# Two feed-forward sublayers of a decoder step, each as seven products of quarters instead of eight

## The chip, the cores and the metric

One core of a Trainium2 chip runs the whole kernel. The metric is the time of one execution on the device in microseconds (us): the median of several runs, lower is better. Beside it stands one profiled execution, from which all durations below are read.

## The reference

One layer of a decoder trunk is computed for 512 prompt tokens and 32 sample tokens (544 columns, handled together). It is a feed-forward sublayer, a mixing sublayer (differential attention and retention side by side), and a second feed-forward sublayer, each followed by a layer norm. The part that matters here is computed twice, with `D_MODEL` = 1024 and `D_FF` = 2816:

```python
def swiglu(x, w_gu, w_down):
    a, u = jnp.split(x @ w_gu, 2, axis=-1)
    return (jax.nn.silu(a) * u) @ w_down

def ffn_sublayer(x, w_gu, w_down, g, b):
    return layer_norm(ALPHA * x + 0.5 * swiglu(x, w_gu, w_down), g, b)
```

## The kernel before

Activations lie with channels on the 128 partitions and the 544 tokens along the free axis (`xT`: 8 tiles of 128 channels). Every large product is done in three passes: weight and activation are each split into a rounded high part (`fp32r`) and the rest, and TensorE (PE) adds high times high, high times low and low times high. A chunk of weights is 256 columns of a matrix and up to 8 tiles of 128 rows, 1 MB. SP loads it (`load_chunk`, line 270) into one of two buffers of `w_raw`, ScalarE (ACT) makes the high part (`split_hi`, line 276), VectorE (DVE) subtracts to get the low part (`split_lo`, line 281), and `gemm` (line 289) multiplies: for each row tile three passes, in each of them one matmul for either half of the tokens (272 columns), into two banks of PSUM. Buffers are handed on by counters: `lo_split` frees the raw chunk, `gemm_done` the split one.

`FFN` (line 315) has two stages. The upper one loops 11 times over a chunk of the gate half and one of the up half of `w_gu`: PE makes two gate tiles and two up tiles, ACT takes the silu of the gate tiles out of PSUM (line 373), DVE multiplies the up tiles by it (line 394), and the product is split again into `hh` and `hl` (lines 377 and 397). The lower one goes through 12 chunks of `w_down`; DVE adds the result, scaled, to `xT` (line 413) and, in the first sublayer, adds the finished tiles into `x_sum` for the norm (line 603). At the end of the first sublayer the next two chunks, those of the projection `pk`, are already loaded and split. GpSimd (POOL) does nothing in either sublayer.

`ChannelNorm` (line 571) follows the first sublayer and the mixing sublayer: PE sums over channels with a matrix of ones (lines 608 and 614), DVE takes a reciprocal (line 642) and scales the 8 tiles (line 646), ACT adds the bias twice, once rounded into `xh` (line 633) and once into `xT` (line 634), and DVE makes `xl` (line 651). The first `gemm` behind it starts on a tile as soon as that tile's `xl` is there. Ahead of the first sublayer `turn_in` turns the input with PE, ACT writes it to `xT` and `xh` (lines 501 and 502) and DVE makes `xl` (line 546). Behind the second one `ln3` turns the result back and stores it.

Each engine runs its own list of instructions in order; an instruction that waits for a counter holds up all that stand behind it on its engine.

## Time and profile before

| | |
|---|---|
| median of 3 runs | 1947.2 us (1946.07 to 1953.2) |
| span of the profiled execution | 1943.7 us |
| matmuls with their records in the trace | 13247 |
| busy: PE, DVE, ACT, POOL | 93%, 40%, 34%, 4% |
| first sublayer, first matmul to last | 27.9 to 426.4 us |
| second sublayer, first matmul to last | 1519.4 to 1921.2 us |

The span runs from the first to the last instruction of the profiled execution; the timed runs have some 3.5 us more at the median. "Busy" is the share of the span in which an engine had at least one instruction running; matmuls overlap one another, so the time of a stream of them is read from its length and its count, not from the duration of one.

### The profile page before, as it was taken

How to read it: one execution, taken by the hardware profiler on the slowest of the kernel's cores; microseconds unless marked ns; L12 is line 12 of the kernel's file. 1: busy time of each engine (PE TensorE's matmuls, PEld its weight loads, DVE VectorE, ACT ScalarE, POOL GpSimd, SP SyncE). 2: the span in 40 equal slices, each digit the busy share in tenths (PEclk: the TensorE clock that was granted, in tenths of full speed). 3: DMA queues.
4: the chain of work that ended last, by engine and by line, in shares of the span. 5: the costliest groups of instructions: out<-in, count | busy, mean ns of one | idle time of the engine just before them, and what ended most of it. 6: DMA issues, size and time to landing. Idle time of an engine off the chain costs nothing.

```text
span 1943.7 us, 33105 instructions
## 1 busy us (share of the span) xinstructions
PE 1804.9 (93%) x13247; PEld 1699.9 (87%) x13247; DVE 778.9 (40%) x1081; ACT 667.4 (34%) x899; POOL 85.2 (4%) x113
## 2 busy tenths in 40 slices
PE   6999999998997768999989999999999899999996
PEld 5999999987997537878768999869998799999996
DVE  2333332234223875756663223344345433333123
ACT  3333331124223555666563222124322433332111
POOL 0000000000002420000000000110000000000002
PEclk9999999999997998999989999999999999999998
DMA  4222222230440015767752232062223022222221
GB/s 142 91 90 91 89 84 82 81 108 22 133 133 23 1 51 176 273 228 249 242 169 91 87 98 84 17 215 66 91 91 100 22 86 87 89 90 84 92 97 46
DMA packets 146659, 203.75 MB, mean 105 GB/s; under 512 B 5538, under 2 KB 127330, under 8 KB 146594
## 3 DMA queue, kind: packets, MB, share of 16 engines
q1 hardware_dynamic: 145442, 198.35, 31.4%
q0 software_dynamic: 1152, 4.46, 0.6%
q8 instruction: 49, 0.80, 0.2%
q14 instruction: 16, 0.13, 0.0%
HBM read 191.39 MB, written 11.40 MB: 104 GB/s over the span
## 4 chain that ended last, share of the span: by engine, by line
PE 88%; DVE 4%; ACT 4%; issue 2%; DMA 0%; SPq 0%; POOL 0%; ACTq 0%; POOLq 0%; DVEq 0%
PE ps L297 68%; PE ps L1201 4%; PE ps L1232 3%; PE ps L1187 2%; PE ps L974 1%; PE ps L988 1%; PE ps L614 1%; PE ps L1624 1%; PE ps L1211 1%; PE ps L1616 1%; PE ps L1248 1%; PE ps L699 1%; PE ps L1198 1%; ACT aT L1069 1%; PE ps L981 0%
## 5 line engine op out<-in xcount | busy, mean ns | idle before, releaser
L297 PE MATMUL ps<-xh,w_hi_t 128*128 128x272 f32 x2432 | 510.1, 291 | 25.3 <-DVE xl L651 18.3
L297 PE MATMUL ps<-xh,w_lo_t 128*128 128x272 f32 x2432 | 505.9, 290 | 0.0
L297 PE MATMUL ps<-xl,w_hi_t 128*128 128x272 f32 x2432 | 504.2, 289 | 0.0
L283 DVE TENSOR_TENSOR w_lo_t<-w_raw,w_hi_t 128x2048 fp32r<-128x2048 f32 (+1 forms) x112 | 252.4, 2254 | 519.2 <-ACT w_hi_t L279 519.2
L297 PEld LDWEIGHTS ps<-xh,w_hi_t 128*128 128x128 f32 x2432 | 385.0, 190 | 30.2 <-issue 20.7
L297 PEld LDWEIGHTS ps<-xl,w_hi_t 128*128 128x128 f32 x2432 | 385.1, 190 | 0.0
L297 PEld LDWEIGHTS ps<-xh,w_lo_t 128*128 128x128 f32 x2432 | 382.4, 190 | 0.0
L279 ACT CAST w_hi_t<-w_raw 128x2048 fp32r<-128x2048 f32 (+1 forms) x112 | 209.9, 1874 | 276.5 <-PE ps L297 276.5
L297 PE MATMUL ps<-hh,w_lo_t 128*128 128x272 f32 x704 | 145.7, 288 | 0.0
L297 PE MATMUL ps<-hh,w_hi_t 128*128 128x272 f32 x704 | 145.5, 288 | 0.0
L297 PE MATMUL ps<-hl,w_hi_t 128*128 128x272 f32 x704 | 145.1, 288 | 0.0
L297 PEld LDWEIGHTS ps<-hh,w_hi_t 128*128 128x128 f32 x704 | 110.7, 188 | 0.0
L297 PEld LDWEIGHTS ps<-hl,w_hi_t 128*128 128x128 f32 x704 | 110.6, 189 | 0.0
L297 PEld LDWEIGHTS ps<-hh,w_lo_t 128*128 128x128 f32 x704 | 109.9, 189 | 0.0
L1303 DVE TENSOR_TENSOR kt_lo<-ps,kt_hi 128x512 fp32r<-128x512 f32 x128 | 82.5, 685 | 57.3 <-ACT kt_hi L1302 57.1
L377 ACT CAST hh<-prod 128x544 f32 x44 | 28.6, 649 | 216.0 <-DVE prod L394 216.0
L1302 ACT CAST kt_hi<-ps 128x512 fp32r<-128x512 f32 x128 | 70.3, 587 | 66.9 <-PE ps L1187 66.7
L1187 PE MATMUL ps<-ident,k_page 128*128 128x128 f32 x512 | 74.8, 285 | 14.1 <-DVE kt_lo L1303 12.4
L1324 DVE TENSOR_TENSOR vp_lo<-v_page,vp_hi 128x1024 fp32r<-128x1024 f32 x64 | 76.4, 1222 | 19.3 <-ACT vp_hi L1320 18.9
L1187 PEld LDWEIGHTS ps<-ident,k_page 128*128 128x128 f32 x512 | 57.5, 144 | 29.1 <-DVE kt_lo L1303 12.8
L394 DVE TENSOR_TENSOR prod<-ps,gated 128x544 f32<-128x544 f32 x44 | 31.9, 725 | 108.2 <-PE ps L297 108.2
L1201 PE MATMUL ps<-kt_hi,q_stat 128*128 128x256 f32 x256 | 71.9, 314 | 0.0
(245 smaller groups left out, 2107.0 us busy)
## 6 DMA issues: line engine op xcount, KB each, us to landing
w_raw<-in_ffn_w_gu_dram SPq DMA_DIRECT2D x44, 1024.0 KB, 5.1
w_raw<-in_w_in_dram SPq DMA_DIRECT2D x32, 1024.0 KB, 5.7
k_page<-in_cache_k_dram SPq DMA_DIRECT2D x64, 512.0 KB, 4.8
v_page<-in_cache_v_dram SPq DMA_DIRECT2D x64, 512.0 KB, 4.6
w_raw<-in_ffn_w_down_dram SPq DMA_DIRECT2D x16, 1024.0 KB, 5.1
w_raw<-in_ffn_w_down_dram SPq DMA_DIRECT2D x8, 768.0 KB, 4.7
w_raw<-in_w_branch_a_dram SPq DMA_DIRECT2D x4, 1024.0 KB, 5.2
st_in<-in_state_ret_dram SPq DMA_DIRECT2D x8, 512.0 KB, 5.0
```

What stands on the lines that cost most here:

```text
L279: nc.scalar.copy(w_hi_t[:, j, 0:nk], w_raw[:, j, 0:nk]).then_inc(hi_split, 1)
L283: nc.vector.tensor_tensor(w_lo_t[:, j, 0:nk], w_raw[:, j, 0:nk], w_hi_t[:, j, 0:nk].bitcast(F32), ALU.subtract).then_inc(lo_split, 1)
L297: mm = nc.tensor.matmul(ps[:, bank + half, 0:HALF], w[:, j, k, w_cols], m[:, k0 + k, half * HALF:half * HALF + HALF], start=start and k == ...
L377: nc.scalar.copy(hh[:, bass.ds(2 * i + n, 1)], prod[:, n:n + 1]).then_inc(self.h_hi, 1)
L394: nc.vector.tensor_tensor(halves(prod[:, n]), banks(4 + 2 * n), halves(gated[:, n]), ALU.mult).then_inc(self.prod_done, 1)
L614: mm = nc.tensor.matmul(ps[:, 2 + a, 0:HALF], ones[:], x_sq[:, k % 2, a * HALF:a * HALF + HALF], start=k == 0, stop=k == KD - 1)
L1187: mm = nc.tensor.transpose(ps[:, half, h * P:h * P + P], k_page[:, g % 4, (4 * half + h) * P:(4 * half + h) * P + P], ident[:])
L1201: mm = nc.tensor.matmul(dst, q_stat[:, P * h:P * h + P], kt[:, q % 2, h], start=False, stop=h == HA - 1 and kt is kt_lo)
L1232: mm = nc.tensor.matmul(ps[:, 6 + half, :], pT[:, g], v[:, g % 2, 512 * half:512 * half + 512], start=g == 0 and v is vp_hi, stop=False)
L1302: return nc.scalar.copy(at_hi, src)
L1303: return nc.vector.tensor_tensor(at_lo, src, at_hi.bitcast(F32), ALU.subtract)
L1324: nc.vector.tensor_tensor(vp_lo[:, g % 2], v_page[:, g % 4], vp_hi[:, g % 2].bitcast(F32), ALU.subtract).then_inc(self.v_lo, 1)
```

## The change

A product of two matrices cut into 2 x 2 quarters normally takes eight products of quarters; Strassen's scheme (here in Winograd's form) takes seven and some additions of quarters. Both sublayers are rewritten in it. A **unit** is 256 columns of weights: 11 `g` units (gate) and 11 `u` units (up), each 1024 rows deep, and 16 `d` units (down) in four groups of four, 2, 3, 3 and 3 pairs of row tiles deep. The quarters of a unit's weights are even and odd row tiles by left and right 128 columns; those of the activations are even and odd row tiles by the two halves of the tokens. The 38 units are worked in the order g0 u0 g1 u1 g2 u2, four d, three pairs, four d, three pairs, four d, two pairs, four d.

A product is 3 passes over 4 (or 2 or 3) row tiles with 272 columns: 12 (6, 9) matmuls into one bank of PSUM. `P1`, `P2`, `P4` take quarters of weights as they are; `P5`, `P6`, `P7`, `P3` take sums of quarters, which POOL makes (`weight_sum`). ACT and DVE split each of the seven into high and low (ring of `SLOTS` = 6). The activations' seven operands are made once per sublayer for g and u (`pool_x`, `act_x`, `dve_x`) and once per pair for d (`hc_hi`, `hc_lo`). Intermediate sums are carried in PSUM and by drains on ACT (copies after P1, P5, P6), DVE (additions after P2, P7, P3, P4) and POOL (the gate's products and the four operand sums after P7 and P3 of a u unit; three additions into `xT` of each d unit). The products of neighbouring units are mixed, so that between a product and the one that needs its drain stand others: for unit n the steady order is P1(n+1) P2(n+1) P7(n) P5(n+1) P3(n) P4(n) P6(n+1). Only the last u unit goes straight into d units that need it.

Besides: `xh` and `xl` are no longer made at the input and by the second `ChannelNorm`; the first two chunks of `pk` are loaded behind the first sublayer, and split inside the norm behind it; the loops of the sublayers are written out.

```diff
+    for lo, hi in ((0, 2), (2, 5), (5, 8), (8, KF // 2)):
+        while pairs < min(hi + 1, KF // 2):
+            units += [("g", pairs, 0, KP), ("u", pairs, 0, KP)]
+            pairs += 1
+        units += [("d", m, lo, hi) for m in range(4)]
...
+            entries += [whole(n + 1, "P1"), whole(n + 1, "P2"), whole(n, "P7"), whole(n + 1, "P5"),
+                        whole(n, "P3"), whole(n, "P4"), whole(n + 1, "P6")]
...
+            def pe_part(self, pe):
+                for e, (n, q, k0, k1) in enumerate(self.entries):
+                    s = self.slot_of[n, q]
+                    pe.wait_ge(self.w_lo, self.s0 + s + 1)
+                    kind, _, lo, _ = self.units[n]
+                    if kind == "d":
+                        pe.wait_ge(self.h_lo, KF // 2 * self.i + k1)
+                    elif n < 2:
+                        pe.wait_ge(self.x_lo, 7 * self.i + B_OF[q] + 1)
...
+                    elif q == "P7":
+                        pe.wait_ge(self.u2_kept, self.n0 + n + 1)
+                        dst = self.x_bank(n)
+                    elif q == "P4":
+                        pe.wait_ge(self.c22, self.n0 + n + 1)
+                        dst = self.x_bank(n)
...
+                        for t, (wt, m) in enumerate(((a_hi, b_hi), (a_hi, b_lo), (a_lo, b_hi))):
+                            mm = nc.tensor.matmul(dst, wt, m, start=opens and k == k0 and t == 0,
+                                                  stop=k == k1 - 1 and t == 2, skip_group_check=True)
+                    mm.then_inc(self.product, 1)
...
+            def weight_sum(self, pool, n, q):
+                self.raw_ready(pool, n)
+                if n:
+                    pool.wait_ge(self.w_lo, self.s0 + self.slot_of[n - 1, P_OF[q]] + 1)
+                out = f_sum[:, int(q) - 1, 0:self.depth(n)]
...
+                    nc.gpsimd.tensor_tensor(out, self.raw(n, 0, 1), self.raw(n, 1, 1), ALU.add).then_inc(self.w_sum, 1)
...
+            def pool_x(self, pool):
...
+                self.x_ready(pool)
+                nc.gpsimd.tensor_tensor(t1, self.quarter(0, 1), self.quarter(0, 0), ALU.subtract).then_inc(self.x_sum4, 1)
...
+                nc.gpsimd.tensor_tensor(t2, self.quarter(1, 1), t1, ALU.subtract).then_inc(self.x_sum4, 1)
...
+                nc.gpsimd.tensor_tensor(t4, self.quarter(1, 0), t2, ALU.subtract).then_inc(self.x_sum4, 1)
+                nc.gpsimd.tensor_tensor(t3, self.quarter(1, 1), self.quarter(0, 1), ALU.subtract).then_inc(self.x_sum4, 1)
...
+            def dve_part(self, dve):
+                for s in range(SLOTS):
+                    self.split_lo(dve, s)
+                self.dve_x(dve)
+                for e in range(len(self.entries)):
+                    self.dve_drain(dve, e)
+                    for p in range(KF // 2):
+                        if e == self.hidden_entry(p, 5):
+                            self.dve_hidden(dve, p)
...
+                    for s in self.split_at[e]:
+                        self.split_lo(dve, s)
...
+            def hidden_entry(self, p, later):
+                e = self.done[self.unit_of["u", p, KP], "P4"] - 1
+                return e if p == KF // 2 - 1 else e + later
...
             def act_part(self, act):
...
+                    self.act_drain(act, e)
+                    for p in range(KF // 2):
+                        if e == self.done[self.unit_of["g", p, KP], "P3"]:
+                            self.act_gate(act, p)
+                        if e == self.hidden_entry(p, 3):
+                            self.act_hidden(act, p)
+                    for s in self.split_at[e]:
+                        self.split_hi(act, s)
...
+                        nc.gpsimd.tensor_tensor(b12[:], b12[:], gate[:, i % 2, 2], ALU.mult).then_inc(self.h_mul, 1)
...
+                        nc.gpsimd.tensor_tensor(t[:, 2], b12[:], t[:, 0], ALU.subtract).then_inc(self.h_sum, 1)
+                        nc.gpsimd.tensor_tensor(t[:, 4], t[:, 6], b12[:], ALU.subtract).then_inc(self.h_sum, 1)
...
+                        nc.gpsimd.tensor_tensor(t[:, 3], t[:, 6], t[:, 2], ALU.subtract).then_inc(self.h_sum, 1)
...
+                        nc.gpsimd.tensor_tensor(t[:, 5], t[:, 1], t[:, 3], ALU.subtract).then_inc(self.h_sum, 1)
...
+                if self.split:
+                    split_hi(act, 0, 0, 0)
+                    split_hi(act, 1, 0, 1)
                 for k in range(KD):
                     act.wait_ge(self.scaled, KD * self.i + k + 1)
...
                 scale(0)
                 scale(1)
+                if self.split:
+                    split_lo(dve, 0, 0)
+                    split_lo(dve, 1, 1)
```

An entry is a product in the list that PE works through. `split_at` gives entry e the splits of the operand six products on, whose place in the ring the product at e has freed; POOL makes the sum for the next unit as soon as the same sum of this unit is split (`weight_sum`). So the operands run five products ahead of PE.

## Rows read from the trace of the kernel before

**Rows 1.** The page, part 1: busy us, share of the span, instructions
```profile
PE 1804.9 (93%) x13247; PEld 1699.9 (87%) x13247; DVE 778.9 (40%) x1081; ACT 667.4 (34%) x899; POOL 85.2 (4%) x113
```

**Rows 2.** The page, part 4: the chain that ended last, by line
```profile
PE ps L297 68%; PE ps L1201 4%; PE ps L1232 3%; PE ps L1187 2%; PE ps L974 1%; PE ps L988 1%; PE ps L614 1%; PE ps L1624 1%; PE ps L1211 1%; PE ps L1616 1%; PE ps L1248 1%; PE ps L699 1%; PE ps L1198 1%; ACT aT L1069 1%; PE ps L981 0%
```

**Rows 3.** The chain in order of time: start us, us, what, times
```profile
27.86 398.54 PE ps L297 x3168
...
565.90 42.10 PE ps L297 x336
...
782.10 1.85 PE ps L1232 x8
...
1529.29 391.90 PE ps L297 x3126
```

**Rows 4.** Stretches of both sublayers: busy us (instructions) by engine, granted clock, DMA
```profile
31.20:426.50 395.30, 395.19 (x3155) 394.97 (x3153) 114.89 (x92) 101.11 (x89) 0.00 (x0) 1.00 0.27 88
1533.00:1921.50 388.50, 388.18 (x3099) 387.96 (x3097) 108.50 (x84) 98.59 (x86) 0.00 (x0) 1.00 0.25 81
```

**Rows 5.** Groups by line and shape, DVE and ACT: busy us, mean ns
```profile
L283 DVE TENSOR_TENSOR w_lo_t<-w_raw,w_hi_t 128x2048 fp32r<-128x2048 f32 x104 | 238.4, 2292 | 448.2 <-ACT w_hi_t L279 448.2
L397 DVE TENSOR_TENSOR hl<-prod,hh 128x544 f32 x44 | 31.9, 726 | 40.9 <-ACT hh L377 40.9
L1668 DVE SCALAR_TENSOR_TENSOR st_out<-st_in,ps 128x256 f32<-128x256 f32 x32 | 11.3, 415 | 23.6 <-PE ps L1624 23.6
L279 ACT CAST w_hi_t<-w_raw 128x2048 fp32r<-128x2048 f32 x104 | 198.0, 1904 | 198.2 <-PE ps L297 198.2
L377 ACT CAST hh<-prod 128x544 f32 x44 | 28.6, 649 | 216.0 <-DVE prod L394 216.0
```

**Rows 6.** Groups by line and shape, POOL
```profile
L568 POOL TENSOR_TENSOR xn<-xn,ln_bias 128x1024 f32<-128x1024 f32 x4 | 9.4, 2345 | 639.8 <-ACT xn L508 639.8
L1691 POOL TENSOR_TENSOR qx<-qrT,cross 128x512 f32<-128x512 f32 x3 | 3.8, 1269 | 6.2 <-PE ps L1587 3.8 <-PE ps L1584 2.4
```

**Rows 7.** Timeline of the attention stage, its start and a later moment: DVE and POOL
```profile
610.57 2.29 DVE L283 TENSOR_TENSOR w_lo_t<-w_raw,w_hi_t 128x2048 fp32r<-128x2048 f32 x1 [9.72 <-ACT w_hi_t L279]
612.78 0.62 DVE L1418 TENSOR_TENSOR qs_lo<-qaT,qs_hi 128x256 fp32r<-128x256 f32 x1
613.32 0.83 DVE L1421 TENSOR_TENSOR kn_lo<-kaT,kn_hi 128x256 fp32r<-128x256 f32 x1
...
610.95 2.17 POOL L958 TENSOR_TENSOR bias<-dist,small 128x128 f32<-128x128 f32 x1 [1.16 <-DVEq L1101]
613.08 0.79 POOL L953 TENSOR_TENSOR q_stage<-qaT,small 128x256 f32<-128x256 f32 x1
613.83 0.58 POOL L958 TENSOR_TENSOR bias<-dist,small 128x128 f32<-128x128 f32 x1
614.45 0.60 POOL L953 TENSOR_TENSOR q_stage<-qaT,small 128x256 f32<-128x256 f32 x1
615.02 0.39 POOL L958 TENSOR_TENSOR bias<-dist,small 128x128 f32<-128x128 f32 x1
...
703.05 0.61 POOL L953 TENSOR_TENSOR q_stage<-qaT,small 128x256 f32<-128x256 f32 x1 [1.72 <-PE ps L974]
...
703.11 0.69 DVE L1020 CUSTOM_DVE_ANT_0 s_sb<-ps,bias 128x512 f32<-128x512 f32 x1
...
703.72 0.69 DVE L1020 CUSTOM_DVE_ANT_0 s_sb<-ps,bias 128x512 f32<-128x512 f32 x1
```

**Rows 8.** Timeline around the second norm: DVE
```profile
1498.58 2.29 DVE L283 TENSOR_TENSOR w_lo_t<-w_raw,w_hi_t 128x2048 fp32r<-128x2048 f32 x1 [0.24 <-ACT w_hi_t L279]
...
1512.71 3.55 DVE L642 RECIPROCAL x_rs<-x_rs 128x544 f32<-128x544 f32 x1 [6.79 <-ACT x_rs L629]
1516.30 1.48 DVE L646 SCALAR_TENSOR_TENSOR xT<-xT,ln_cols,x_rs 128x544 f32<-128x544 f32 x2
```

**Rows 9.** Timeline around the first norm: DVE
```profile
443.33 3.55 DVE L642 RECIPROCAL x_rs<-x_rs 128x544 f32<-128x544 f32 x1 [7.47 <-ACT x_rs L629]
446.92 1.48 DVE L646 SCALAR_TENSOR_TENSOR xT<-xT,ln_cols,x_rs 128x544 f32<-128x544 f32 x2
...
449.15 0.73 DVE L651 TENSOR_TENSOR xl<-xT,xh 128x544 fp32r<-128x544 f32 x1 [0.76 <-ACT xT L634]
```

**Rows 10.** Timeline at the start: the input's way through ACT
```profile
20.00 1.01 ACT L501 COPY xT<-ps 128x1024 f32<-128x1024 f32 x1 [0.22 <-PE ps L474]
20.91 1.02 ACT L502 CAST xh<-ps 128x1024 fp32r<-128x1024 f32 x1
```

**Rows 11.** The page, part 6: DMA issues, KB each, median us to landing
```profile
w_raw<-in_ffn_w_gu_dram SPq DMA_DIRECT2D x44, 1024.0 KB, 5.1
v_page<-in_cache_v_dram SPq DMA_DIRECT2D x64, 512.0 KB, 4.6
```

More of the change, by code:

```diff
@@ L263, in build @@
         out_stored = sem("out_stored")
+        rows_landed = [sem(f"rows_landed{j}") for j in range(4)]
         def score_ps(row):
@@ new lines, in build @@
+            raw_in = [sem(f"f_raw_in{j}") for j in range(RAWS)]
+            w_sum, w_hi, w_lo = sem("f_w_sum"), sem("f_w_hi"), sem("f_w_lo")
+            product = sem("f_product")
+            x_sum4, x_hi, x_lo = sem("f_x_sum"), sem("f_x_hi"), sem("f_x_lo")
+            u1_kept, p5_kept, u2_kept = sem("f_u1_kept"), sem("f_p5_kept"), sem("f_u2_kept")
+            c11, c22, c12 = sem("f_c11"), sem("f_c22"), sem("f_c12")
+            c21_act, c21_dve = sem("f_c21_act"), sem("f_c21_dve")
+            gated = sem("f_gated")
@@ new lines, in build @@
+            h_mul, h_sum, h_hi, h_lo = sem("f_h_mul"), sem("f_h_sum"), sem("f_h_hi"), sem("f_h_lo")
+            added = sem("f_added")
+            units, entries = ffn_plan()
+            N = len(units)
+            slot_of, done = {}, {}
+            for e, (n, q, _, _) in enumerate(entries):
+                slot_of.setdefault((n, q), len(slot_of))
+                done[n, q] = e + 1
+            slots = list(slot_of)
+            sum_of = {(0, q): j + 1 for j, q in enumerate("1234")}
+            for n, q in slots:
+                if q in SUM_OF and n + 1 < N:
+                    sum_of[n + 1, SUM_OF[q]] = len(sum_of) + 1
@@ new lines, in build @@
+            split_at = [[] for _ in entries]
+            for s in range(SLOTS, len(slots)):
+                e = max(done[slots[s - SLOTS]] - 1, max([k for k, got in enumerate(split_at) if got], default=0))
+                split_at[e].append(s)
+            c21_of, n_act, n_dve, d_of = {}, 0, 0, {}
+            for n, unit in enumerate(units):
+                if unit[0] == "g":
+                    n_act += 1
+                    c21_of[n] = n_act
+                else:
+                    n_dve += 1
+                    c21_of[n] = n_dve
+                if unit[0] == "d":
+                    d_of[n] = len(d_of)
@@ new lines, in build, with __init__ @@
+            added_of = {}
+            for n, q, _, k1 in entries:
+                if n in d_of and q in ("P2", "P7", "P3") and k1 == units[n][3]:
+                    added_of[n, q] = len(added_of) + 1
+            unit_of = {(u[0], u[1], u[3]): n for n, u in enumerate(units)}
+            def __init__(self, index, w_gu, w_down, x_ready, free, norm=None):
+                self.i, self.gu, self.down = index, w_gu, w_down
+                self.x_ready, self.free, self.norm = x_ready, free, norm
+                self.n0, self.p0, self.s0 = self.N * index, len(self.entries) * index, len(self.slots) * index
@@ new lines, in kind, with depth, made, c21_read @@
+            def kind(self, n):
+                return self.units[n][0]
+            def depth(self, n):
+                return self.units[n][3] - self.units[n][2]
+            def made(self, eng, n, q):
+                eng.wait_ge(self.product, self.p0 + self.done[n, q])
+            def c21_read(self, eng, n):
+                if self.kind(n) == "g":
+                    eng.wait_ge(self.c21_act, self.n_act * self.i + self.c21_of[n])
+                else:
+                    eng.wait_ge(self.c21_dve, self.n_dve * self.i + self.c21_of[n])
@@ new lines, in hidden_free, with out @@
+            def hidden_free(self, eng, p):
+                if p >= PAIRS:
+                    part = next(u for u in self.units if u[0] == "d" and u[2] <= p - PAIRS < u[3])
+                    self.made(eng, self.unit_of["d", 3, part[3]], "P4")
+            def out(self, n, c):
+                kind, i, _, _ = self.units[n]
+                j = {"11": 0, "22": 1, "12": 2}[c]
+                if kind == "g":
+                    return gate[:, i % 2, j]
+                if kind == "u":
+                    return b12[:] if c == "12" else hc_raw[:, i % PAIRS, {"11": 0, "22": 6}[c]]
+                return self.scratch(n, j)
@@ L1542, in __init__ @@
                 self.s_sc_set = sem("rs_sc_set")
-                self.s_in = [sem(f"rs_in{j}") for j in range(4)]
+                self.s_in = rows_landed
                 self.s_qm_zero = sem("rs_qm_zero")
@@ L1799, in act_part @@
             def act_part(self, act):
-                with act.Fori(0, 2) as i:
-                    for j in range(2):
-                        split_hi(act, self.c + 2 * i + j + 2, self.c // 2 + i + 1, j)
+                for j in range(2):
+                    split_hi(act, self.c + j + 2, self.c // 2 + 1, j)
             def dve_part(self, dve):
@@ L1842, in build @@
         out_proj = OutProject(C_OUT)
-        ln2 = ChannelNorm(1)
-        ffn2 = FFN(1, C_FFN2_UP, ffn2_w_gu, ffn2_w_down, last=True)
-        ln3 = Norm(2, 0, 1, back=False)
+        ln2 = ChannelNorm(1, split=False)
+        ffn2 = FFN(1, ffn2_w_gu, ffn2_w_down, ln2.ready, lambda eng: eng.wait_ge(gemm_done, 2 * C_END + 4))
+        ln3 = Norm(2)
         att_const = sem("att_const")
@@ L2082, in _ @@
             ln2.pe_part(pe)
-            ffn2.pe_part(pe, lambda k: ln2.ready(pe, k))
-            pe.wait_ge(ffn2.resid, 2 * KD + 4)
+            ffn2.pe_part(pe)
+            for m in range(4):
+                ffn2.settled(pe, m)
             ln3.pe_part(pe)
```

611 lines of the change are left out of this document (391 added, 220 removed).

## The prediction, made before the changed kernel ran

> **What bounds the kernel now.** I read the page first: PE is busy 93% of the span, DVE 40%, ACT 34%, POOL 4% [rows 1], and line 297, the large products, is 68% of the chain that ended last [rows 2]. The chain in order of time shows both sublayers as one unbroken piece of PE each: 3168 matmuls in 398.5 us and 3126 records in 391.9 us [rows 3], so 0.1254 us for each at full pace (391.9 / 3126). Over these stretches the granted clock is 1.00, the 2.4 GHz level, DVE and ACT work 29% and 26% of the time and POOL not at all [rows 4]. So PE's count of matmuls sets both sublayers, some 797 of 1943.7 us, and fewer matmuls are worth time as long as the others keep up. That is the question, because the change gives them more.
>
> **What is removed.** A unit g or u took 96 matmuls and takes 84, a pair of row tiles of a d block 24 and now 21. A sublayer goes from 3168 to 22 x 84 + 4 x 11 x 21 = 2772, so 396 x 0.1254 = 49.7 us less for either, 99.3 us together. Two doubts about PE cost next to nothing. Twelve matmuls in a row now go into one bank: line 1232 does that, with 512 columns, in 0.231 us each (1.85 / 8), 0.45 ns a column, as 0.1254 us for 272 is 0.46 [rows 3]. And the code is unrolled: `pq`, unrolled too, runs 336 matmuls in 42.1 us, 0.1253 each [rows 3].
>
> **What is added.** Prices, from groups with the same operands [rows 5, 6]:
> - DVE with two SBUF inputs: 2048 elements 2.29 us, 544 0.73; in between 0.16 + 1.04 ns each, so 512 (a split) 0.69, 384 0.56, 256 0.43, 1088 1.29, 1904 (the hidden operands of a pair) 2.14. DVE with one PSUM input, 256 elements 0.415; the drains of 272 I take at 0.4, as they overlap a little.
> - ACT: 2048 1.90, 544 0.65, so 0.20 + 0.83 ns: 512 0.62 (0.55 in a row), 272 0.4, 1904 1.8, 816 0.87.
> - POOL with two full inputs: 1024 2.35, 512 1.27, so 0.19 + 2.10 ns: 384 1.00, 272 0.76, 256 0.73, 1088 2.48.
>
> PE needs 10.5 us for a unit g or u (84 x 0.1254), 7.9 for a d unit 3 deep, 5.3 for one 2 deep. Taken alone every engine fits: for g and u DVE 7.5 us, ACT 6.5, POOL 4 x 1.27 + 3.5 x 0.76 = 7.7. The loads fit too: 1 MB in 5.1 us [rows 11], asked for about a unit ahead.
>
> **DVE and POOL exclude each other.** This decides the sum, and the trace has one place that shows it [rows 7]. POOL's line 958 takes 0.39 us when left alone (615.02). At 610.95 it begins beside a split of DVE and takes 2.17: it ends at 613.12, 0.26 behind the end of the split (612.86). DVE's next subtraction of 256 elements ends at 613.40, 0.28 behind that, instead of taking 0.43; then POOL at 613.87, DVE at 614.15, POOL at 614.41. Each waits for the other to finish a whole instruction, in turn. What is held is the price less a start of 0.14 us: POOL 1.13 for 512, 0.86, 0.62 (272), 0.59, 2.34; DVE 0.55, 0.42, 0.28, 1.15, 2.0. Drains out of PSUM go free: line 1020, with one input there, takes 0.69 beside POOL (703.11) as alone (703.72).
>
> The Trainium skill, "SBUF — State Buffer", section "Who interferes with whom", says that a DVE instruction with two SBUF inputs and a GpSimd instruction that reads SBUF lock each other out through a shared read port, while one with a single SBUF input does not; the first half agrees with the 2.17 us [rows 7], and by the page's reading the sum below holds, without it the first rival does.
>
> Held time, which has to follow one after the other:
> - pair g + u: POOL 8 x 1.13 + 7 x 0.62 = 13.4, DVE 14 x 0.55 + 2.0 = 9.7: 23.1 us, against 21.1 of PE and 24.1 before (192 x 0.1254).
> - d 3 deep: 4 x 0.86 + 3 x 0.62 + 7 x 0.42 = 8.2, against 7.9 and 9.0 before. 2 deep: 4 x 0.59 + 1.86 + 7 x 0.28 = 6.2, against 5.3 and 6.0.
>
> So not PE sets the pace but this pair of engines. Nor can they fill every moment. I laid two pairs out, each instruction at the price above behind what it waits for. POOL's burst of a u unit (two products, five operations, three sums) makes DVE wait for one of them at every split. The last operand sum comes 7 us behind P4 of u; ACT, in order, waits for it with `act_hidden` and its next split behind it; DVE waits for that split, and behind it stands the addition after P7, for which PE waits at P4: 1.4 us in the u unit, 2.0 in the g unit. A pair comes to 24.6 us, 1.5 over the held time; one d unit to 8.7 and 6.7. Stream of a sublayer: 11 x 24.6 + 12 x 8.7 + 4 x 6.7 = 401.8, less 3 for the first pair, which starts without arrears, plus 2 for the larger sums of g and u made beside the shallow d: 401, against 397.3 (3168 x 0.1254). **+4 each, +8.** From below the bound is the held time filled without gaps, 11 x 23.1 + 12 x 8.2 + 4 x 6.2 = 377; from above, whole prices one behind the other (13.4, 9.9, 7.9 a unit), 445.
>
> **Ends and joints.**
> - From u10 into the d units PE has no other work, where before it had no gap [rows 3]. Behind P4: POOL's five operations, in arrears by 3 us, end 6.5 us later, then the cast 1.8, DVE's subtraction 2.1: 10.5 us, of which 1.5 come back as arrears are made up. **+18** for both; without arrears 6.7 each.
> - Start of the second sublayer. Before, PE began behind the reciprocal (ended 1516.26 [rows 8]) while tiles were still coming; had it run at full pace it would have begun at 1529.29 - 42 x 0.1254 = 1524.0, 7.8 us behind it. After: eight tiles scaled and biased to +6.6, six splits on ACT to +9.8, then POOL's four sums of activations (2.34 held) and DVE's seven splits of them (1.15 held) in turn: the fifth operand, for P7, is there at +27.9, with six products (9.0 us) done by then. 27.9 - 9.0 - 7.8 = **+11**; if they didn't exclude each other +6.
> - Start of the first: ACT's copies take a tile each 1.0 us less [rows 10], so x is ready at 22.3; by the same steps P7 starts at 43.6, so 43.6 - 9.0 = 34.6 against 29.1 before (27.86 + 398.54 - 397.3 [rows 3]). **+5.5**; PE will be idle in between, and if it gets the 1.2 GHz level for that, up to 3 more.
> - First norm into `pk`: two weight chunks are split inside it. ACT's two casts (3.8) lie beside the reciprocal (3.55 [rows 9]) and cost nothing; DVE's two (4.5) go before the first `xl`, which began 0.75 us behind the scaling [rows 9], so 3.75 late, less 0.85 for the split that used to stand before the centring. Their loads are queued on SP behind the end of the sublayer and take 2 x 5.1 us, hidden by 20 us of norm. **+2.9.** DVE's eight additions for the norm now compete in the last d units: **+2**. Second norm: one split less before it [rows 8], **-0.5**.
> - The end keeps its length: the last drains are shorter, POOL's lie beside P4.
>
> Sum: 8 + 18 + 11 + 5.5 + 2.9 + 2 - 0.5 = +47 on 1943.7, so a span of 1990.6; the runs' median stands 3.5 above the span: **1994 us**, 2.4% slower. (A measurement of this kernel can tell some 0.5% from no change, 1937.5 to 1957.)
>
> **The rivals.**
> - *They hardly meet* (faster). If the exclusion is rare in practice, PE sets the pace: -99.3, + 2 x 6.7 at u10, + 1 and + 6 at the starts, + 2.4 at the norms, + 7 for stalls behind the hidden casts in the shallow d units: -69.5, 1878 us. For it: each engine alone has a third of its time free. Against it: every split and every POOL operation here is of the kind in rows 7. 0.17.
> - *They meet but fill every moment*: 377 instead of 401 (-20 each instead of +4), u10 +13, starts +12, norms +2.4: -13, 1934 us; with some of the gaps, up to 1957. For it: arrears of five products are allowed for. Against it: P4 waits for the addition two products behind P7. 0.15, half of it within 0.5%.
> - *It doesn't even reach turn-taking* (slower still): whole prices in sequence, 445 a sublayer, +96 and +40 for the rest: 2083 us. It decides if an engine never has its next instruction waiting when the other lets go; rows 7 show it waiting each time. 0.05.
> - That fewer products are computed by count is plain from the code; no chance for that.
>
> **How the numbers follow.** The forecast has 0.63: 1957 to 2045, from gaps half as large to twice as large (3 us a pair more is +66). The most likely time is 1994. The range 1905 to 2045 leaves out the first rival, the third, and little else. Faster by over 0.5%: 0.17 + 0.07 = 0.24; within: 0.08 + 0.02 of the forecast's lower edge = 0.10; slower: 0.66.
>
> **What would show it.** PE busy in the sublayers falls from 100% to about 86%, with some 5540 matmuls at 0.125 us inside a product. PE's waits are on DVE's additions (`c22`, before P4) and, at u10, on the hidden split. DVE's splits of 512 elements show 0.9 to 1.8 us instead of 0.69, and POOL's sums more than 1.27; if they read 0.69 and 1.27, the forecast is wrong and the first rival right. A pair takes 24.6 us from P1 to P1; the gap behind the last P4 of u is 10 us; the second sublayer's P7 starts 28 us behind the reciprocal.

## The result, and the profile after

The changed kernel takes 2054.2 us (2053.1 to 2055.7, four runs) against 1950.2 before: 1.053 times as long, interval 1.0505 to 1.0554. The direction was forecast, the size was not: +47 us on the span were expected, 110 came (2053.9 against 1943.7), and 2054 lies 9 us above the range.

The page of after: busy time by engine, PE and POOL in 40 slices, and the chain by engine (before: [rows 1, 2]).

```profile
PE 1761.9 (86%) x12455; PEld 1637.9 (80%) x12455; DVE 1261.4 (61%) x1746; ACT 874.5 (43%) x1550; POOL 748.5 (36%) x675
...
PE   4979898876999776999989999899995888889885
...
POOL 4777777761100430000000000210002677777765
...
PE 61%; DVE 16%; issue 10%; ACT 6%; POOL 6%; DMA 0%; SPq 0%; ACTq 0%; POOLq 0%; DVEq 0%
```

PE has 792 matmuls fewer, and POOL is now busy 36% of the span instead of 4%, nearly all of the added time in the sublayers. There the chain no longer stays on PE; it runs through DVE, ACT and POOL as well. The two stretches from the seventh product (P7 of the first unit) to the last matmul of a sublayer, after (length, then busy us and instructions of PE, PEld, DVE, ACT, POOL, granted clock, DMA; before: [rows 4]):

```profile
52.00:475.90 423.90, 361.06 (x2702) 351.25 (x2700) 335.10 (x414) 198.12 (x401) 306.96 (x269) 0.97 0.23 75
1610.80:2031.70 420.90, 361.06 (x2702) 351.75 (x2700) 330.42 (x408) 198.08 (x400) 306.34 (x269) 0.97 0.24 78
```

PE is busy 85% (361.06 / 423.90). The forecast had 86%, but that the two agree is luck: 2702 matmuls at 0.1254 us are 339 us, or 80%. The rest is time at a lower clock (0.97 granted, 1.00 before) and, at each wait, a last matmul whose record is longer than its share of a stream (0.29 against 0.126 us).

The next rows are DVE's splits (count; minimum, median and maximum in ns) and POOL's sums (busy us, mean ns) after; in the timeline, POOL takes 1.27 us for such a sum while DVE is idle, and DVE 0.68 for a split.

```profile
L557 DVE TENSOR_TENSOR f_lo<-f_sum,f_hi x176: 675/1142/1783, 24.9 to 1980.1; 128x512 fp32r<-128x512 f32 x176
L557 DVE TENSOR_TENSOR f_lo<-f_raw,f_hi x132: 676/896/1777, 23.7 to 1981.5; 128x512 fp32r<-128x512 f32 x132
...
L579 POOL TENSOR_TENSOR f_sum<-f_raw,f_sum 128x512 f32<-128x512 f32 x44 | 67.4, 1532 | 5.5 <-POOL f_sum L567 4.8 <-issue 0.7
L572 POOL TENSOR_TENSOR f_sum<-f_sum,f_raw 128x512 f32<-128x512 f32 x44 | 58.3, 1326 | 23.9 <-DVE f_lo L557 19.1 <-DVE f_lo L554 3.0 <-POOL f_sum L579 1.0
```

The splits begin at 0.68 us (the 0.69 of the sum) and reach 1.78, which is one POOL sum held (1.13) and one split held (0.55) on top of a tenth; the sums are at 1.33 to 1.53 instead of 1.27. So the splits and sums take as long as the exclusion priced them. Where the other 63 us come from, by the forecast's own terms (times of the first and last matmuls of products and sublayers in both traces):

| term | forecast, us | measured | over |
|---|---|---|---|
| first sublayer: P7 of unit 0 starts at | 43.6 | 52.0 | +8.4 |
| first sublayer: from there to its last matmul | 403.3 | 423.9 | +20.6 |
| first norm into `pk` | +2.9 | +3.9 | +1.0 |
| `pk` to the end of the output projection (unchanged code) | 0 | +8.8 | +8.8 |
| second norm up to its reciprocal | -0.5 | -3.0 | -2.5 |
| second sublayer: P7 behind the reciprocal | 27.9 | 35.5 | +7.6 |
| second sublayer: from there to its last matmul | 401.0 | 420.8 | +19.8 |
| end | 0 | -0.3 | -0.3 |

(403.3 is 426.4 of before + 5.5 + 4 + 9 + 2 - 43.6; 401.0 is 404.9 from reciprocal to last matmul before + 11 + 4 + 9 - 27.9.) Measured from P1 to P1, the inner pairs take 23.7 and 24.0 us in the mean (forecast 24.6), but a d unit 3 deep 10.9 (8.7) and one 2 deep 9.1 and 8.6 (6.7). In a group 3 deep the four come as 10.3, 13.2, 9.6 and 10.6 us. (The last group, behind u10, is left out of these means.)

One thing the sum had only at the starts is the clock. 0.03 short of full speed is 24 to 25 us at the 1.2 GHz level in each sublayer from P7 on, most of it in the groups of d units, where PE waits most. Three pairs in a row of after, and then a group of four d units, as above:

```profile
143.50:214.00 70.50, 63.10 (x487) 61.95 (x487) 57.97 (x66) 34.60 (x67) 51.93 (x41) 0.99 0.25 83
214.00:257.60 43.60, 35.88 (x264) 34.53 (x263) 35.07 (x45) 19.35 (x42) 34.61 (x32) 0.96 0.26 85
```

88 and 94 matmuls begin at that level in the two sublayers. They start 0.23 us apart instead of 0.126, some 9 us more of PE's time in each sublayer; how much of it lies on the path, inside the 20 us of the table, no run separates.

What goes on in a d unit of after, from 242.7 us on: ACT, DVE and POOL.

```profile
245.92 0.39 ACT L715 COPY gate<-ps 128x272 f32<-128x272 f32 x1 [3.68 <-POOL xT L776]
246.21 1.35 ACT L545 ACTIVATE f_hi<-f_sum 128x384 fp32r<-128x384 f32 x3
...
244.44 0.76 DVE L554 SCALAR_TENSOR_TENSOR f_lo<-f_raw,f_hi 128x384 fp32r<-128x384 f32 x1
246.77 0.56 DVE L554 SCALAR_TENSOR_TENSOR f_lo<-f_sum,f_hi 128x384 fp32r<-128x384 f32 x1 [1.56 <-ACT f_hi L545]
...
242.75 1.01 POOL L572 TENSOR_TENSOR f_sum<-f_sum,f_raw 128x384 f32<-128x384 f32 x1 [0.55 <-DVE f_lo L554]
243.72 1.07 POOL L764 TENSOR_TENSOR xT<-xT,gate 128x272 f32<-128x272 f32 x1
244.75 1.08 POOL L776 TENSOR_TENSOR xT<-xT,gate 128x272 f32<-128x272 f32 x1
247.47 1.01 POOL L575 TENSOR_TENSOR f_sum<-f_raw 128x384 f32<-128x384 f32 x1 [1.63 <-DVE f_lo L554]
```

ACT's drain of P5 (line 715) stands 3.68 us for POOL's addition of the unit before (776), because the scratch it writes is read there. Three splits queue behind the drain, DVE idles 1.56 us for them, POOL idles 1.63 us for DVE. That is a ring of three in-order queues, and no step of the sum had it.

### The profile page after: what moved, and what is told of

Read it like the earlier page. It is cut to its first block, busy times and chain, and to the rows that moved or that the text cites. A ratio compares the mean times of both kernels' runs of the same rounds, so it can differ in the third digit from the quotient of the medians.

```text
span 2053.9 us, 34447 instructions
## 1 busy us (share of the span) xinstructions
PE 1761.9 (86%) x12455; PEld 1637.9 (80%) x12455; DVE 1261.4 (61%) x1746; ACT 874.5 (43%) x1550; POOL 748.5 (36%) x675
## 4 chain that ended last, share of the span: by engine, by line
PE 61%; DVE 16%; issue 10%; ACT 6%; POOL 6%; DMA 0%; SPq 0%; ACTq 0%; POOLq 0%; DVEq 0%
PE ps L338 26%; PE ps L525 16%; DVE f_lo L557 4%; DVE f_lo L554 4%; PE ps L1570 3%; PE ps L1601 3%; PE ps L1556 2%; DVE hc_lo L664 2%; PE ps L1343 2%; ACT f_hi L545 1%; PE ps L1357 1%; DVE gate L643 1%; PE ps L1617 1%; PE ps L975 1%; PE ps L1995 1%
## 5 line engine op out<-in xcount | busy, mean ns | idle before, releaser
L525 PE MATMUL ps<-xc_hi,f_hi 128*128 128x272 f32 x1232 | 364.7, 296 | 83.0 <-DVE xc_lo L612 35.2
L525 PE MATMUL ps<-xc_hi,f_lo 128*128 128x272 f32 x1232 | 360.6, 293 | 0.0
L525 PE MATMUL ps<-xc_lo,f_hi 128*128 128x272 f32 x1232 | 359.2, 292 | 0.0
L525 PEld LDWEIGHTS ps<-xc_hi,f_hi 128*128 128x128 f32 x1232 | 236.4, 192 | 93.0 <-issue 46.9
L525 PEld LDWEIGHTS ps<-xc_lo,f_hi 128*128 128x128 f32 x1232 | 236.6, 192 | 0.0
L525 PEld LDWEIGHTS ps<-xc_hi,f_lo 128*128 128x128 f32 x1232 | 236.2, 192 | 0.0
L338 PE MATMUL ps<-xh,w_hi_t 128*128 128x272 f32 x1024 | 217.5, 294 | 15.0 <-DVE xl L1016 12.9
L338 PE MATMUL ps<-xh,w_lo_t 128*128 128x272 f32 x1024 | 214.4, 291 | 0.0
L338 PE MATMUL ps<-xl,w_hi_t 128*128 128x272 f32 x1024 | 213.7, 291 | 0.0
L338 PEld LDWEIGHTS ps<-xl,w_hi_t 128*128 128x128 f32 x1024 | 163.4, 191 | 0.0
```

The lines of the kernel that those rows point to most:

```text
L338: mm = nc.tensor.matmul(ps[:, bank + half, 0:HALF], w[:, j, k, w_cols], m[:, k0 + k, half * HALF:half * HALF + HALF], start=start and k == ...
L525: mm = nc.tensor.matmul(dst, wt, m, start=opens and k == k0 and t == 0, stop=k == k1 - 1 and t == 2, skip_group_check=True)
```

## The experiments

All are edits of the changed kernel unless said otherwise; `...` marks what is left out. Spans are from single profiled executions, and the times of runs 1 to 8 and 11 to 14 are single runs.

**1. Two sets of scratch in the d units.**

```diff
 def scratch(self, n, j):
+    if self.units[n][1] % 2:
+        return gate[:, (self.last_pair(n) + 1) % 2, 3] if j == 2 else spare[:, j]
     return gate[:, (self.last_pair(n) + 1) % 2, j]
```

> The d units use two sets of scratch banks in SBUF by turns (odd row tiles: three spare buffers), so that ACT's drains of one unit no longer wait for POOL's additions of the unit before; nothing else is changed. Theory (a ring: drain on ACT waits for POOL, the splits queue behind the drain on ACT, DVE waits for the splits, POOL's next sum waits for DVE): the d units fall from 10.6 us (3 deep) and 9.1 (2 deep) to the 8.7 and 6.7 of the sum, so 12 x 1.9 + 4 x 2.4 = 32 us less for a sublayer, 64 for both: about 1990 us. Rival (DVE and POOL excluding each other set the d units alone, with whole prices of 9.9 and 7.9 us): within 10 us of 2054, with POOL's waits moved elsewhere.

2031.4 us, span 2029.6: 23 less, where 64 were expected. From P7 to the last matmul 414.9 and 411.4 us: 9.0 and 9.4 less, and the wait named above is gone (the drain now waits 0.54 us, for PE). PE's waits in the first sublayer (52 to 475 us; what it waited for: us, times, longest), after and then with two sets:

```profile
PE ps L525 <- DVE gate L643: 39.9, 25, 3.8
PE ps L525 <- ACT gate L722: 7.9, 10, 1.7
PE ps L525 <- DVE hc_lo L664: 7.0, 1, 7.0
```

```profile
PE ps L535 <- DVE gate L653: 30.5, 17, 3.8
PE ps L535 <- DVE spare L653: 10.0, 7, 2.6
PE ps L535 <- DVE hc_lo L674: 7.0, 1, 7.0
```

PE's 7.9 us for ACT's drain are gone from its longest waits, but the 40 us for DVE's addition (`gate` and `spare` together) have not fallen. The ring is real, and about half of the 20 us; d units still take 10.6 us (3 deep) and 8.7 and 8.3 (2 deep), not 8.7 and 6.7.

**2. Weight sums on DVE.**

```diff
-    nc.gpsimd.tensor_tensor(out, self.raw(n, 0, 1), self.raw(n, 1, 1), ALU.add).then_inc(self.w_sum, 1)
+    nc.vector.tensor_tensor(out, self.raw(n, 0, 1), self.raw(n, 1, 1), ALU.add).then_inc(self.w_sum, 1)
 ...
 for s in self.split_at[e]:
     self.split_lo(dve, s)
+    self.sum_after(dve, s)
```

> The four sums of weights of each unit are made by DVE, right behind the split that frees their place, instead of by POOL; POOL keeps the hidden products and sums, the additions into x and the sums of x. Theory (DVE and POOL exclude each other, so what counts is the time that either holds): a sum of 512 holds 0.55 us on DVE and 1.13 on POOL, so a pair's held time falls from 23.1 to 18.5 us, below the 21.1 of PE, and POOL no longer lags in the d units. Pairs come to some 21.6 us (23.8 now), d units to 8.2 and 6.3: 24 + 39 us less for a sublayer, about 1925 us in all. Rival (they hardly hinder each other, DVE is simply busy): 16 us of DVE for a pair become 21 or more, nothing is gained: 2050 or more.

2010.2 us: 44 less, where 129 were expected. Giving DVE more work does make the kernel faster. That is what a shared resource would do; by itself it would also fit a POOL that is merely late, which run 4 tests. Pairs fell to 22.3 us, but the d units of a group to 9.6, 12.9, 8.8 and 9.6 only, 10.2 in the mean. By the prediction's prices the two engines now hold each other for 18.5 us a pair and 6.5 a d unit (4 x 0.42 + 3 x 0.62 + 7 x 0.42), less than PE's 21.1 and 7.9, and yet PE waits. A likely reason, not shown, is DVE's own list: seven splits, four sums and four drains of 3-deep tiles are 11 x 0.56 + 4 x 0.42 = 7.8 us, beside POOL's additions and the ring.

The Trainium skill, "GPSIMD Engine Reference", section "Elementwise — side-by-side cycle accounting", gives an addition of 2048 elements on GpSimd as 1.96 times as long as on VectorE; here, each alone, 512 elements take 1.27 against 0.69 us, 1.8 times.

**3 and 4. The weight sums left out, and replaced by writes that read nothing.**

```diff
-    nc.gpsimd.tensor_tensor(out, self.raw(n, 0, 1), self.raw(n, 1, 1), ALU.add).then_inc(self.w_sum, 1)
+    nc.gpsimd.memset(out, 0.5).then_inc(self.filled, 1)
+    pool.wait_ge(self.filled, c)
+    nc.gpsimd.memset(out, 0.5).then_inc(self.w_sum, 1)
```

> POOL's four sums of weights of each unit are left out but for one column: a lower bound, f_sum holds a constant. Theory: held time of a pair 14 us, of a d unit under 5, so PE sets the pace: pairs 21.2 us, d units 8.0 and 5.6, 70 us less for a sublayer, about 1905 us; DVE's splits come down to 0.69 us but for those beside POOL's hidden operations. Rival (the sums cost nothing on the path, the ring of scratch and drains alone makes the d units long): the d units keep 10 and 9 us, about 2000 us.

> In place of each of POOL's four sums of weights of a unit POOL writes a constant twice over the same place, about as long (1.1 us for 512) without reading anything; the sums themselves are left out. Theory (it is POOL's reading of SBUF beside DVE's that costs): as with the sums left out, within 15 us of that kernel, some 1910 us, DVE's splits near 0.69 us. Rival (POOL's occupancy costs: its queue is late, whatever it does there): pairs of 23 us and d units of 10, 2030 to 2054 us.

1931.0 and 1952.9 us: 123 and 101 less than the changed kernel. Both kernels leave the sums out, so they show times alone. With the writes, POOL is held up nearly as long for each sum (2 x 0.53 us, where a sum alone takes 1.27), but DVE's splits run at their price. From the kernel with writes, POOL's group and DVE's splits:

```profile
L575 POOL MEMSET f_sum<- 128x512 f32 x176 | 92.6, 526 | 10.1
...
L558 DVE TENSOR_TENSOR f_lo<-f_sum,f_hi x176: 680/692/1276, 24.9 to 1882.1; 128x512 fp32r<-128x512 f32 x176
```

A median of 692 ns instead of 1142. So it is POOL's reading beside DVE's that costs, some four fifths of what the sums cost in all; the other 22 us, where at most 15 were expected between the two kernels, come with POOL's time itself. By the Trainium skill, "SBUF — State Buffer", section "Who interferes with whom", a two-input DVE instruction contends with a GpSimd instruction that reads SBUF and not with one that only writes it; the 692 ns agree. Both forecasts were 26 and 43 us too low: the starts, the gap at u10 and the first d units of a group (9.1 us) remain.

**5. The hidden cast and subtraction later.**

```diff
-if e == self.hidden_entry(p, 5):
+if e == self.hidden_entry(p, 9):
     self.dve_hidden(dve, p)
 ...
-if e == self.hidden_entry(p, 3):
+if e == self.hidden_entry(p, 7):
     self.act_hidden(act, p)
```

> One edit to the changed kernel: the cast of a pair's hidden operands on ACT is placed 7 products behind the pair's last one instead of 3, and DVE's subtraction for it 9 instead of 5 (not for the last pair of a sublayer, where it is needed at once). Theory (ACT, in order, stands up to 8 us before this cast, waiting for POOL's last hidden sum, and the splits of weights queue behind it): the second d unit of a group falls from 13.2 us to about 10 and pairs lose some of their 2.6 us over PE's 21.1, say 1 each: 3 x 3 + 11 x 1 = 20 us less for a sublayer, about 2015 us. Rival (ACT's wait only shows that POOL is late, and PE waits for POOL and DVE anyhow): the same time within 8 us, with the idle time moved to other units.

2100.4 us, 46 more. The edit was too large: the pair before the last is wanted by the next d unit nine products later, and PE stood there. From this kernel, PE's first matmul of a group of d units:

```profile
222.03 0.57 PE L525 MATMUL ps<-hc_hi,f_hi 128*128 128x272 f32 x1 [6.36 <-issue]
```

DVE's subtraction for that pair ends at 221.92. Apart from that, the second d unit fell from 13.2 to 7.9 us, further than the 10 of the theory, and the third rose from 9.6 to 14.1: in a group nothing was won. That speaks for the rival, in a run that is spoilt by the other effect.

**6. The start in another order.**

```diff
 for q in "1234":
     self.weight_sum(pool, 0, q)
+self.pool_x(pool)
 for s in range(SLOTS):
     self.pool_after(pool, s)
-self.pool_x(pool)
 ...
     nc.scalar.copy(xc_hi[:, j], self.b_operand(j)).then_inc(self.x_hi, 1)
+    if j == 3:
+        self.act_drain(act, 0)
```

> One edit to the changed kernel, at the start of both sublayers only: POOL makes the four sums of x ahead of the two sums of weights of the second unit, and ACT drains the first product behind the fourth of its seven casts of x instead of behind the last. Theory (the sixth and seventh product were late because both of these were in the way, steps that my sum had left out): the seventh product starts some 8 us earlier in both sublayers (43.6 us instead of 52.0 in the first, 27 behind the reciprocal instead of 35 in the second): about 2038 us. Rival (the start is bound by POOL and DVE taking turns on the sums and splits of x, whatever the order): 2050 or more.

2060.2 us, no gain. In the first sublayer P7 starts at 50.1 instead of 52.0 us, but P1 at 39.7 instead of 33.2: POOL's sums of x went first, and DVE's six weight splits, in turn with them, lasted until 38.3. In the second sublayer P7 is 1.8 us earlier against the end of the output projection (50.6 against 52.4 behind it). The streams behind it took 2.3 and 2.1 us longer, and the unchanged code between the sublayers 3.7. The rival holds for these two moves together: the order only moves which operand is late. The drain alone was not tried.

**7. Sums on DVE, two sets of scratch and hidden casts later, together.** The edits of 1, 2 and 5.

> Three edits together: weight sums on DVE, two sets of scratch in the d units, hidden casts later. Alone the first took 44 us and the second 23. Theory (each takes another part of the same ring, and with all three neither POOL nor ACT holds a d unit up, so what is left is PE's 21.1 us a pair and DVE's own work): pairs 21.4, d units 8.3 and 6.5 in a group, about 1925 us. Rival (DVE, now with all splits and sums, is the bound: 7 splits, 4 sums and 4 drains of a d unit are some 8.5 us alone, and 9.5 beside POOL): d units stay at 9.5 or more, about 1965 us.

2053.4 us. The third edit spoils it as in run 5 (the last u unit before a group takes 17.7 us instead of 12.3). **12. The same without the third:**

> Weight sums on DVE and two sets of scratch together, hidden casts where the change has them: the three edits of the run before without the one that cost time. Theory (scratch holds the d units up also where POOL no longer makes sums): the 20 us of two scratches come on top of the 44 of the sums on DVE, about 1990 us. Rival (with the sums on DVE, POOL has its additions done in time, or DVE's own work is the bound): 2005 or more.

1997.2 us. From P7 to the last matmul 395.3 and 391.5 us, against 404.7 and 400.4 with the sums on DVE alone: 9.4 and 8.9 less, the same 9 us a sublayer as in run 1; the start, where P7 came 2.7 us later, took some back: 13 us in all, between the two forecasts. The ring is apart from who makes the sums.

**8. The kernel before, again.** No edit.

> The kernel before, unchanged, for a second trace of it: the stretch between the two sublayers (first product of the first projection to the last of the output projection) took 1046.3 us in its first trace and 1051.4 to 1056.6 in five traces of kernels with the change, whose code in this stretch is the same. If it takes over 1051 here, those 5 to 10 us are a spread of executions and no part of what the change costs; if it takes 1046 again, the change has a cost there that no step of the sum names.

1047.7 us for that stretch, nearly as in the first trace. The windows of the stretch in both traces of before (the second fence is the second trace), after and in run 7; the last numbers of a row are the granted clock, the DMA share and GB/s:

```profile
450.00:1496.30 1046.30, 967.29 (x6757) 874.51 (x6758) 491.73 (x816) 414.19 (x656) 73.31 (x104) 0.96 0.37 122
```

```profile
450.60:1498.30 1047.70, 969.88 (x6758) 875.58 (x6758) 491.85 (x816) 414.44 (x656) 73.47 (x104) 0.96 0.37 121
```

```profile
503.30:1558.40 1055.10, 977.31 (x6757) 883.62 (x6758) 489.91 (x815) 413.53 (x656) 73.38 (x104) 0.95 0.37 119
```

```profile
498.50:1562.10 1063.60, 984.72 (x6758) 886.89 (x6758) 489.37 (x815) 413.63 (x656) 73.55 (x104) 0.94 0.36 118
```

DVE, ACT and POOL do the same in all four; PE takes longer, and its granted clock is lower: 0.04, 0.05 and 0.06 short of full speed are 84, 106 and 128 us at the 1.2 GHz level. The 8.8 us of the table go with this clock; that it causes them is likely, and what lowers it is not shown.

**9, 10 and 11. Only half of the change.** The units g and u keep seven products; the d units are computed plainly, eight products of quarters into four PSUM banks that DVE adds to x, four hidden operands instead of seven, no sums for d. In run 11 that is all; in run 9 the remaining weight sums are on DVE; in run 10 the sums of x are too, and ACT drains the first product behind its fourth cast of x.

```diff
+products = ("000", "001", "010", "011", "100", "101", "110", "111")
 ...
+        if kind == "d" and units[n][0] == "d":
+            entries += [whole(n + 1, q) for q in products]
 ...
+                elif q in ("100", "101", "110", "111"):
 ...
+                    nc.vector.tensor_tensor(x, x, bank(n), ALU.add).then_inc(sig, 1)
```

> Only half of the change: the units g and u keep their seven products, the d units are computed plainly (eight products of quarters, accumulated in four PSUM banks, drained by DVE straight into x; four hidden operands instead of seven, no sums for d), and the weight sums of g and u are made by DVE. Theory (DVE and POOL are one resource, and the d units overfill it: their seven splits, four sums and three additions for 1.1 us of PE saved each): held time of a pair 15 us, of a d unit 4, PE sets the pace, pairs 21.2 us, d units 9.0 and 6.0: 366 us a sublayer against 397 before; starts as in the kernel with sums on DVE (10 and 17 us later than before), norm 4, u10 about 1: about 1920 us, faster than before by 1.3%. Rival (pairs stay at 22.3 us, as with the sums on DVE, because DVE alone is too busy there): 24 us more, 1945, no gain over before.

> As the kernel with plain d units, and at the start of a sublayer the four sums of x are made by DVE (1.2 us each) instead of POOL (2.3 held), two of them ahead of the splits of x, with ACT's drain of the first product behind its fourth cast of x. Theory (at the start too it is the time held in turn that counts): the seventh product starts some 7 us earlier in the first sublayer and 10 in the second, 17 us below the kernel with plain d units, about 1903 us. Rival (the start waits for ACT's casts or the loads): within 5 us of it.

> Plain d units as in the first kernel of this call, but the weight sums of g and u stay on POOL: the change without its d half and with nothing else moved. Theory: held time of a pair is 19.8 us (eight sums, three products, fourteen splits, a hidden subtraction of 1088 elements), under PE's 21.1 but close, so pairs of 21.8 us and d units of 9.1 and 6.1; starts and norms as in the changed kernel: about 1940 us. Rival (POOL's lag from the sums carries over into the d units as before): pairs of 23 and d units of 10, 1975 us.

1920.5, 1917.3 and 1927.9 us against 1951.7 before. Run 9 came as forecast. Runs 9 and 10 are 0.984 (0.9815 to 0.9869) and 0.982 (0.9795 to 0.9845) of before, so faster than both kernels, than the one before by 1.6 and 1.8%. Run 11 beats its own forecast by 12 us. Its chain, and its windows from P7 to the last matmul:

```profile
59.95 314.94 PE ps L542 x2499
```

```profile
51.80:410.00 358.20, 357.28 (x2834) 356.87 (x2832) 255.90 (x367) 160.81 (x305) 145.94 (x113) 1.00 0.28 89
1545.60:1903.80 358.20, 357.30 (x2834) 356.89 (x2832) 248.70 (x358) 160.62 (x304) 145.58 (x113) 1.00 0.29 92
```

PE is unbroken for 2499 matmuls, at 0.1260 us each and at full clock. A pair takes 21.2 us although POOL still makes its eight sums and the two engines hold each other, by the prediction's prices, for 19.8 of every 21.1 us: here they cost nothing, where I had allowed 0.7 us for gaps. At most three such pairs follow one another; the d units between them hold little more than four splits (4 x 0.42 = 1.7 of 9.1 us), so that what is late can catch up. In run 10 P7 came 4.1 us earlier than in run 9, and in the second sublayer 5.7 us earlier against the end of the output projection, but unit 1 then took 15.0 us instead of 11.9 (14.1 instead of 11.7), and what was left were 1.4 and 4.3 us: the rival.

**13 and 14. P4 one product later**, alone and with two sets of scratch.

```diff
-                        whole(n, "P3"), whole(n, "P4"), whole(n + 1, "P6")]
+                        whole(n, "P3"), whole(n + 1, "P6"), whole(n, "P4")]
```

> One edit to the changed kernel: in the order of products P4 of a unit and P6 of the next one are exchanged (but at the last pair), so that three products instead of two lie between P7 and P4, which waits for DVE's addition behind P7 (the addition into c22). In the trace of the changed kernel PE stands 50 us a sublayer before P4 (13.7 in g, 6.5 in u, 8.7 in the d units 2 deep, 21.5 in those 3 deep, some 1.8 us for each). Theory of latency (the addition is only some turns of DVE late, more products in between hide it): about 1.1 us less for most of 37 units, 30 us a sublayer, about 1995 us. Theory of the shared resource (DVE and POOL are filled, the wait before P4 is where that shows, and if it isn't there it shows before another product): within 12 us of 2054.

> The same exchange together with two sets of scratch in the d units (2031 us alone). Theory of latency: the two add up, 60 us less for P4 and 20 for scratch, about 1975 us. Theory of the shared resource: 2018 to 2035 us, the d units 3 deep at 10 us or more in the mean.

2067.1 and 2020.8 us, 13 more and 33 less than the changed kernel. PE's waits in the first sublayer of run 13 and then of run 14, as above:

```profile
PE ps L525 <- ACT gate L722: 31.9, 13, 5.6
...
PE ps L525 <- DVE gate L643: 3.3, 6, 1.3
```

```profile
PE ps L535 <- ACT gate L732: 7.4, 3, 2.7
PE ps L535 <- DVE hc_lo L674: 7.0, 1, 7.0
PE ps L535 <- DVE spare L653: 4.9, 7, 1.5
```

Alone, the 40 us for DVE's addition fell to 3, and the wait came back before P7, on ACT's drain of P6 into the scratch (8 to 32 us), and before P1: from P7 to the last matmul 429.0 us, 5 more. With the second scratch the drain has no such wait, and the stretch takes 405.5 and 403.8 us, where the forecast had 403.3 and 401.0. So neither theory holds alone: the wait before P4 is no latency that can be taken away by itself, and yet the shared resource was not full, since both edits together give 18.4 and 17.0 us. (The time of run 14 lies in the range of the second theory, but its d units 3 deep take 9.5 us, not the 10 or more that came with it.)

## Why the prediction was right and wrong, point by point

- **PE's saving**: right. 792 matmuls fewer over both sublayers, and where PE sets the pace (run 11) 0.126 us for each.
- **Exclusion and held times**: right, in kind (run 4, and run 2 fits it) and price. The four sums of x beside splits of 1088 elements come 3.5 us apart (the next fence's splits), which is 2.34 + 1.15.
- **Stream, +4 each**: wrong by 20, and this is the step that failed. The gaps on top of the held times were mis-sized, in the d units. I had laid out two pairs and carried their gaps over to the d units (0.5 us each), without laying out a d unit. Measured, a d unit stands 2.7 us over its held time (10.9 - 8.2), 2 deep 2.9 and 2.4; the pairs, at 23.7 and 24.0 us, came out 0.9 and 0.6 below the forecast. The wait before P4 was in the sum, but in the wrong units: 1.4 us in u and 2.0 in g, where 0.6 and 1.2 came, and at most the 0.5 in a d unit, where 1.9 came (6.5 and 13.7 us in 11 units each, 30.2 in 16). A d unit's scratch is single (9 us a sublayer, run 1), and P4 follows only two short products behind P7 and waits for DVE's addition (another 9 and 8, run 14 against run 1, once the scratch is double). The first of these is a wait that the change adds, behind which splits are queued: the code had it, and I priced POOL's addition but not who waits for it. With both changed, the stretch is within 2.2 and 2.8 us of the forecast (run 14), but that does not prove the sum: d units still take 9.5 and 8.0 us (8.7 and 6.7), pairs 23.9 (24.6), and the errors offset each other. And the held times are only a lower bound (run 2).
- **Starts, +5.5 and +11**: wrong by 8 each. The operand of P7 came nearly when forecast: 44.9 us (43.6), and 28.3 behind the reciprocal (27.9). But "with six products done by then" failed: P6 writes the bank of P1, and ACT's drain of P1 stood behind seven casts of x, of which the fifth waits for POOL's last sum. The start of the first sublayer, after: DVE's splits of x, ACT and PE.

```profile
32.99 3.60 DVE L612 TENSOR_TENSOR xc_lo<-xT,xc_hi 128x1088 fp32r<-128x1088 f32 x1
36.51 3.60 DVE L612 TENSOR_TENSOR xc_lo<-xc_raw,xc_hi 128x1088 fp32r<-128x1088 f32 x1
...
42.52 2.10 ACT L605 CAST xc_hi<-xc_raw 128x1088 fp32r<-128x1088 f32 x2 [5.96 <-POOL xc_raw L595]
44.53 1.09 ACT L605 CAST xc_hi<-xT 128x1088 fp32r<-128x1088 f32 x1
45.53 0.38 ACT L711 COPY gate<-ps 128x272 f32<-128x272 f32 x1
...
46.05 0.56 PE L525 MATMUL ps<-xc_hi,f_hi 128*128 128x272 f32 x1 [4.06 <-ACT gate L711]
```

  So P6 began at 46.05 and three products, the first at the 1.2 GHz level (2.86 us to the start of the next instead of 1.51), still lay before P7. Run 6 moved the drain together with POOL's sums, without profit.
- **u10, +9 each**: right in size, in part by luck. The first d unit there takes 19.6 us, 9.3 more than where a group begins elsewhere (10.3). The gap behind P4 alone is 7.0 us instead of 10, near the 6.7 that the prediction gave without arrears: POOL has none here and, undisturbed, needs 0.77 us for each of the last operations. Behind the gap 15 matmuls run at the 1.2 GHz level, some 1.5 us more, which the term did not have. Plain d units bring the unit to 14.7 against 13.6 elsewhere (run 11).
- **Norms**: the first right, +3.9 for 2.9; the second -3.0 for -0.5. The first sublayer, with DVE's additions for its norm, is 3.1 us longer than the second (423.9 - 420.8), for 2; no run takes these additions out.
- **Unchanged code, 0**: wrong by 8.8, along with a lower granted clock (run 8). Without it the kernel would have been at the edge of the range.
- **Rivals.** *They hardly meet* is refuted by the splits' median of 1142 ns and run 4, *fill every moment* by run 14: even without the two waits a sublayer stays at 405.5 us from P7, where that rival gave 377 (403.3 - 24 - 2.5). *Whole prices* (2083 us) is by the number nearer to 2054 than the forecast is, and gave 9.9 us for a d unit, near the 10.9, but by a mechanism that isn't there: the pairs, at 23.8, were below the forecast, and it gave them 26.8.

What stays open: why the 1.2 GHz level comes more often between the sublayers in all kernels with the change, how much of the 20 us it makes up inside them, why d units still take 10 us with the sums on DVE, and how much of a start could be won with another design.

## What to carry to other kernels

Where two engines exclude each other, sum what they hold of the shared resource and compare it with the bound engine's time. Over it, the bound engine waits, and work that is taken away or given to the engine that does it in less helps most. Under it they can cost nothing (run 11: 19.8 of 21.1 us), but need not: in runs 2 and 12 the pairs held 18.5 and took 22.3 and 22.0. Moving a wait helped only once its buffer was double (run 13 lost 13 us, run 14 won 33). So lay out by hand the unit with the least slack, not the longest one, and ask of each drain into a single buffer who reads it last and what is queued behind the drain. A change made of two halves should be priced by halves: here the d half, with four sums, seven splits and seven drains for 1.1 us of PE, costs 126 us on top of the other (2054.2 - 1927.9), where the other half alone wins 24 on the kernel before.

## What had not been expected of the hardware

- A stretch with the same code took 1046 to 1064 us in different kernels, with the granted clock between 0.96 and 0.94 and the other engines' busy time the same within 0.5%. The time of this kernel carries some 10 us that go with the clock of an unedited stage.
- Two engines in turn on one resource, 94% filled in the pairs (19.8 / 21.1, by the prediction's prices) and little used between groups of at most three, left PE without a single gap for 2499 matmuls.
